# A hybrid decoder layer on Trainium2: modulation chunks computed inside the projections, and another order of the prompt attention inside the sample attention

## The chip, the cores and the metric

The kernel runs on one core of a Trainium2 chip. The metric is the device time of one execution in microseconds (us). Its engines are TensorE (PE, with its weight loads as PEld), VectorE (DVE), ScalarE (ACT), GpSimd (POOL) and SyncE (SP), which here only issues transfers. Sixteen DMA engines move the data.

## What is computed

One layer for a prompt of 512 tokens and, beside it, for 8 sequences of 8 sample tokens with 2048 cached positions each. The width is 1024.

```python
mod = (jax.nn.silu(c) @ w_ada + b_ada).reshape(B, 6, 1, D_MODEL)
shift1, scale1, gate1, shift2, scale2, gate2 = [mod[:, i] for i in range(6)]
h = x * (1 + scale1) + shift1
proj = h @ w_in                      # 1024 x 3072: qa, ka, va, qb, kb, vb
qa, ka, qb, kb = rope(...)           # 64 columns per head
oa, win_state = attend_a(qa, ka, va)
ob = rms_norm(attend_b(qb, kb, vb, lam), subln_g) * (1.0 - lam_init)
mixed = concat(oa, ob) @ w_o
x = layer_norm(ALPHA * x + gate1 * mixed)
h = x * (1 + scale2) + shift2
x = layer_norm(ALPHA * x + gate2 * conv_ffn(h))
```

`attend_a` has 8 heads of 64; each query sees keys at three patterns of window and dilation, (128, 1), (512, 4) and (2048, 16), and the three results are mixed by their softmax sums. `attend_b` has 4 heads with two query and key maps of 64 and a value of 128: softmax(q1 k1) v minus lambda times softmax(q2 k2) v. The sample tokens read window caches (A) and a paged cache through a page table (B). The window caches, shifted by 8 rows, are outputs too: 16 copies from memory to memory (keys and values of 8 sequences), 4 MB each.

## The kernel before

All engines are programmed by hand, each with its own list of instructions, in order; they wait for one another by semaphores. `x_sb`, `ht`, `ring` and `room` are large regions of on-chip memory, each divided anew stage by stage; `wide` is the matmul output memory, `bk(i)` one of its eight banks of 512 columns.

**Weights** are cut into 37 chunks of 2 MB (128 partitions x 8 x 512), listed in `CHUNKS` (L42), and go through slots of `ring` by `SLOT_OF` (L44). SyncE loads them with `load_chunk` (L460, the transfer at L482), which waits until the slot's last chunk is used. A chunk of `w_ada` gives 512 of the 6144 modulation columns, for 9 rows of c. TensorE multiplies it in `ada_rows` (L1516; eight matmuls of 512 columns, L1524), VectorE copies the product (L1026), TensorE sums and transposes it in `ada_sum` (L1528; four matmuls of 9 columns, L1536), VectorE adds the bias (L1031).

**Stage 1, projections.** After modulation chunks 0 to 3 (shift and scale of the first half) come 30 units (s, t): six chunks s of `w_in` by five token tiles t (4 of the prompt, 1 of the sample). TensorE does a unit in `product` (L1573 to L1577), in three parts because numbers are split into a high part and a rest; VectorE and GpSimd split the weights (L1065 to L1080 and L701), VectorE rotates queries and keys (rope, L1122), GpSimd adds (L715). TensorE transposes queries and keys (L1626); ScalarE copies the queries into `qtp` (L834), where each head has its own 128 rows of which 64 are zero (GpSimd writes the zeros at the start, L673), and the values into `vp` (L827). SyncE walks the units too: it stores the new keys and values (L536, L540, L551, L554), and after the last tile of a chunk loads the next `w_in` chunk and, for the first three, copies a window pair (`move_window`, L515 to L517); one more pair is copied ahead of the units. When the units are done it loads modulation chunks 4 to 11 through three ring slots.

**Stage 2, prompt attention of head group A.** A unit is a head and a block of 128 queries: 32 units for A, in a pipeline of four steps: scores (TensorE, L1636), mask and minimum (VectorE, L1164), exponential (ScalarE, L844), transposes (TensorE, L1643), copy (VectorE, L1172), weighing with the values (TensorE, L1649), scaling (VectorE, L1183). In steps with s % 4 == 3 stands an `ada_rows`, in those behind them the `ada_sum`:

```python
if s % 4 == 0 and s >= 4:
    ada_sum(4 + s // 4 - 1)
...
if s < NU and s % 4 == 3:
    ada_rows(4 + s // 4)
```

In the last four steps VectorE begins to turn (transpose in blocks of 32, `turn_keys`, L1148) the key groups of the first window.

**Stage 3, sample attention.** 16 windows w: for each of 8 sequences first cache A (3 groups), then cache B (4 groups). SyncE and GpSimd's queue bring key groups into 3 buffers (`kraw`, L589, L592, L596) and value groups into 4 (`vg`, L445, L453). The 8 new rows of keys and values of a window lie in `kn` and `vn`, two buffers each, loaded by `load_new` (L422 to L426): for windows 0 and 1 by ScalarE when the prompt attention is over, later by SyncE. VectorE turns them in `turn_new` (L1230). TensorE scores each group (`score_group`, L1700), VectorE takes minima, ScalarE exponentials, and `weigh_group` (L1732) sums. Between them lie the 32 prompt units of head group B, two for each window, in three parts on each engine: `scores_b`, `turn_b`, `weigh_b` (TensorE, L1674 to L1687), `mask_b`, `out_b` (VectorE, L1203 to L1224), `probs_b`, `copy_b` (ScalarE, L853 to L869). Their order is written out in the loop over the windows: scores of unit 2w at the start, transposes of 2w and scores of 2w + 1 after value group 2, weighing of 2w and transposes of 2w + 1 at the end, weighing of 2w + 1 at the start of the next.

**After it**: the norm of B's rows, the output projection, both layer norms, and the ConvFFN, with the remaining window copies.

## Time and profile before

| | us |
|---|---|
| median of 3 runs | 1243.8 (1243.23 to 1244.69) |
| the profiled execution | 1241.13 |
| its span, first to last instruction | 1239.0 |
| TensorE busy | 1055.3 (85%) |
| VectorE busy | 838.9 (68%) |
| GpSimd busy | 358.1 (29%) |
| ScalarE busy | 269.6 (22%) |
| moved by DMA | 276.5 MB, mean 223 GB/s |

The profile is that of one execution. Its busy shares are averages over the span; the page's slices and the windows of the trace give them by stretch, with the granted TensorE clock (1.00 is 2.4 GHz, 0.50 is 1.2 GHz). The stages lie at 0 to 51.8 (start and first modulation), 51.8 to 237.1 (projections), 237.1 to 310.4 (prompt attention of group A), 310.4 to 649.6 (sample attention) and from there to 1239.0.

### The profile page before, as it was taken

How to read it: one execution, taken by the hardware profiler on the slowest of the kernel's cores; microseconds unless marked ns; L12 is line 12 of the kernel's file. 1: busy time of each engine (PE TensorE's matmuls, PEld its weight loads, DVE VectorE, ACT ScalarE, POOL GpSimd, SP SyncE). 2: the span in 40 equal slices, each digit the busy share in tenths (PEclk: the TensorE clock that was granted, in tenths of full speed). 3: DMA queues.
4: the chain of work that ended last, by engine and by line, in shares of the span. 5: the costliest groups of instructions: out<-in, count | busy, mean ns of one | idle time of the engine just before them, and what ended most of it. 6: DMA issues, size and time to landing. Idle time of an engine off the chain costs nothing.

```text
span 1239.0 us, 24009 instructions
## 1 busy us (share of the span) xinstructions
PE 1055.3 (85%) x9389; PEld 851.3 (69%) x9389; DVE 838.9 (68%) x1521; ACT 269.6 (22%) x588; POOL 358.1 (29%) x378
## 2 busy tenths in 40 slices
PE   4599999999577777766785996999999999999994
PEld 2377777666455545554564875999999999777772
DVE  1657457267766757685749477477676676998958
ACT  0310010232223223232333103322332232100002
POOL 2433243100000000000007005366565565434323
PEclk9799999999788679799876996999999999999997
DMA  8958894686999999999990206366567731412202
GB/s 301 403 185 303 309 370 145 215 302 225 318 325 339 313 346 302 343 331 350 301 334 17 64 26 221 121 252 238 204 221 285 269 107 69 148 56 97 73 22 77
DMA packets 112549, 276.54 MB, mean 223 GB/s; under 512 B 9608, under 2 KB 33174, under 8 KB 108837
## 3 DMA queue, kind: packets, MB, share of 16 engines
q1 hardware_dynamic: 99125, 250.82, 59.8%
q10 hardware_dynamic: 13312, 24.19, 5.5%
q8 instruction: 75, 1.23, 0.4%
q14 instruction: 37, 0.30, 0.1%
HBM read 264.60 MB, written 76.69 MB: 275 GB/s over the span
## 4 chain that ended last, share of the span: by engine, by line
PE 61%; DVE 21%; DMA 9%; issue 4%; SPq 3%; POOL 2%; ACT 1%; ACTq 0%; DVEq 0%; POOLq 0%; PEldq 0%
PE wide L1575 16%; PE wide L1577 15%; PE wide L1576 15%; DMA ring<-in_cache_k 5%; DVE ring L1148 5%; PE wide L1649 3%; PE wide L1638 2%; DMA ring<-in_w_ada 2%; PE wide L1700 2%; DVE ring_r L1080 2%; PE wide L1732 1%; PE wide L1524 1%; DMA ring<-in_w_down 1%; PE wide L1754 1%; PE wide L1643 1%
## 5 line engine op out<-in xcount | busy, mean ns | idle before, releaser
L744 POOL TENSOR_TENSOR ring_r<-ring,ring_r 128x1024 fp32r<-128x1024 f32 x70 | 185.2, 2654 | 271.1 <-DVE ring_r L1040 204.2
L1575 PE MATMUL wide<-x_sb_r,ring_r 128*128 128x288 f32 x704 | 211.4, 300 | 8.2 <-DVE ht_r L1062 5.1
L1576 PE MATMUL wide<-ht_r,ring_r 128*128 128x288 f32 x704 | 209.3, 297 | 0.0
L1577 PE MATMUL wide<-x_sb_r,ring_r 128*128 128x288 f32 x704 | 208.7, 296 | 0.0
L1577 PE MATMUL wide<-ring_r,ht_r 128*128 128x512 f32 (+1 forms) x400 | 158.9, 397 | 0.0
L1148 DVE STREAM_TRANSPOSE ring<-ring 128x512 f32<-128x512 f32 x208 | 129.2, 674 | 30.4 <-DMA ring<-in_cache_k 30.4
L1575 PEld LDWEIGHTS wide<-x_sb_r,ring_r 128*128 128x128 f32 x704 | 133.4, 189 | 11.7 <-issue 11.2
L1577 PEld LDWEIGHTS wide<-x_sb_r,ring_r 128*128 128x128 f32 x704 | 134.2, 191 | 0.0
L1576 PEld LDWEIGHTS wide<-ht_r,ring_r 128*128 128x128 f32 x704 | 133.7, 190 | 0.0
L1700 PE MATMUL wide<-ring,x_sb 128*32 128x128 f32 (+1 forms) x1792 | 70.2, 309 | 50.5 <-DVE ring L1148 50.4
L1575 PE MATMUL wide<-ring_r,x_sb_r 128*128 128x512 f32 (+1 forms) x240 | 97.7, 407 | 12.1 <-DVE ht_r L1062 10.1
L1700 PEld LDWEIGHTS wide<-ring,x_sb 128*32 128x32 f32 x1792 | 52.9, 127 | 69.7 <-DVE ring L1148 61.6
L726 POOL COPY x_sb<-ring 32x128 f32<-32x128 f32 x64 | 18.4, 287 | 269.0 <-PE wide L1700 266.8
L1576 PE MATMUL wide<-ring_r,x_sb_r 128*128 128x512 f32 (+1 forms) x240 | 94.9, 395 | 0.0
L1575 PE MATMUL wide<-ring_r,ht_r 128*128 128x512 f32 (+1 forms) x220 | 88.1, 400 | 4.4 <-DVE ht_r L1400 2.5
L1577 PEld LDWEIGHTS wide<-ring_r,ht_r 128*128 128x128 f32 (+1 forms) x400 | 72.4, 181 | 21.5
L1576 PE MATMUL wide<-ring_r,ht_r 128*128 128x512 f32 (+1 forms) x220 | 86.6, 394 | 0.0
L1414 DVE SCALAR_TENSOR_TENSOR room<-room,vec_t 128x512 f32<-128x512 f32 x44 | 56.9, 1294 | 40.4 <-ACT room L957 40.2
L949 ACT ACTIVATE room<-wide,vec_t 128x576 f32<-128x576 f32 x44 | 32.8, 744 | 205.9 <-PE wide L1577 201.2
L1416 DVE SCALAR_TENSOR_TENSOR room<-room,vec_t 128x512 f32<-128x512 f32 x44 | 71.5, 1625 | 1.6
L1040 DVE CAST ring_r<-ring 128x1024 fp32r<-128x1024 f32 x62 | 41.9, 687 | 35.9 <-DMA ring<-in_w_up 29.4
L1649 PE MATMUL wide<-room 128*128 128x128 f32 x320 | 57.2, 315 | 9.6 <-ACT room L869 8.4
(225 smaller groups left out, 1889.0 us busy)
## 6 DMA issues: line engine op xcount, KB each, us to landing
ring<-in_cache_k SPq DMA_DIRECT2D x128, 256.0 KB
out_wks<-in_cache_win_k SPq DMA_DIRECT2D x8, 4080.0 KB, 19.0
out_wvs<-in_cache_win_v SPq DMA_DIRECT2D x8, 4080.0 KB, 24.8
ring<-in_w_ada SPq DMA_DIRECT2D x12, 2048.0 KB, 10.2
ring<-in_w_up SPq DMA_DIRECT2D x22, 1024.0 KB, 7.3
ring<-in_cache_win_k SPq DMA_DIRECT2D x16, 1024.0 KB
ring<-in_w_in SPq DMA_DIRECT2D x6, 2048.0 KB, 18.5
room<-in_cache_v ACTq DMA_DIRECT2D x32, 256.0 KB
```

The lines of the kernel that those rows point to most:

```text
L744: nc.gpsimd.tensor_tensor(rest, w, high.bitcast(F32), ALU.subtract).then_inc(wl_rest, 1)
L949: nc.scalar.activation(u_b[:, k % 2, 2:2 + NT].rearrange("p (h t) -> p h t", h=2), pair, ACT.Identity, bias=vec_t[:, 0, 48 + f:49 + f]).th ...
L1040: nc.vector.tensor_copy(pair_of(n, slice(k, k + 2))[0], slot(SLOT_OF[n])[:, k:k + 2, :]).then_inc(wl_high, 1)
L1080: nc.vector.tensor_tensor(rest, w, high.bitcast(F32), ALU.subtract).then_inc(win_dve, 1)
L1148: last = nc.vector.transpose(ktg[:, G % NK, :, 32 * t:32 * t + 32], kraw[G % NK][:, t, :].rearrange("p (g d) -> p g d", d=32))
L1414: then(nc.vector.scalar_tensor_tensor(out=c_p, in0=u_b[:, k % 2, 1:1 + SEQ], scalar=tap(1), in1=c_p, op0=ALU.mult, op1=ALU.add))
L1416: nc.vector.scalar_tensor_tensor(out=c_p, in0=u_b[:, k % 2, 0:SEQ], scalar=tap(0), in1=c_p, op0=ALU.mult, op1=ALU.add)
L1575: nc.tensor.matmul(out, left[0], right[0], start=first, stop=False)
L1576: nc.tensor.matmul(out, left[0], right[1], start=False, stop=False)
L1577: return nc.tensor.matmul(out, left[1], right[0], start=False, stop=last)
L1649: last = nc.tensor.matmul(bank[:, 0:P], pt_b[:, u % 2, P * kb:P * kb + P], vp[:, kb, m, P * (n // 2):P * (n // 2) + P], start=(kb == 0), s ...
L1700: last = nc.tensor.matmul(bank[32 * nn:32 * nn + 32, at:at + nk], qbd[:, w % 2, g].rearrange("p i q -> p (i q)"), keys[:, g, 0:nk], start= ...
```

## The change

- The eight late modulation chunks leave the weights ring and the prompt attention. They go one after the other through a buffer of their own, `late`, in `room`, and their products stand ahead of units 3, 6, 10, 13, 16, 20, 23 and 26 of the projections (`LATE_UNIT`), each sum one unit later. SyncE asks for a chunk with `load_late` once the product before has been made, after the stores of the unit at which that product stands.
- The 8 window copies of the projections are spread singly over the units (`COPY_UNIT`).
- The queries lie in `qt` with two heads' 64 rows one above the other; scores are made with 64 rows. The 8192-column memset goes, ScalarE copies a tile's queries with one instruction. The space gives `late` its place, and value buffers 2 and 3 of the sample attention lie there afterwards.
- `kn`, `vn` and `ktn` have one buffer each. The first window's new rows are loaded by ScalarE ahead of its first exponential, those of later windows by SyncE, keys and values by separate steps.
- As before 32 prompt units (group A) precede the sample attention and 32 (group B) lie in it, but there each of the 34 `prompt_step(y)` does the weighing of y - 2, the transposes of y - 1 and the scores of y, at the start of a window and after its value group 1. ScalarE's and VectorE's parts move accordingly.

```diff
-CHUNKS = [("ada", i) for i in range(4)] + [("in", i) for i in range(6)] + [("ada", i) for i in range(4, 12)] \
+CHUNKS = [("ada", i) for i in range(4)] + [("in", i) for i in range(6)] \
     + [("o", i) for i in range(2)] + [("up", i) for i in range(11)] + [("down", i) for i in range(6)]
-SLOT_OF = [0, 1, 2, 3] + [0, 1] * 3 + [0, 1, 2, 0, 1, 2, 0, 1] + [i % 2 for i in range(19)]
+SLOT_OF = [0, 1, 2, 3] + [0, 1] * 3 + [i % 2 for i in range(19)]
...
+LATE_UNIT = {4: 3, 5: 6, 6: 10, 7: 13, 8: 16, 9: 20, 10: 23, 11: 26}
+COPY_UNIT = {1: (0, "k"), 4: (0, "v"), 8: (1, "k"), 11: (1, "v"), 14: (2, "k"), 18: (2, "v"), 21: (3, "k"), 24: (3, "v")}
...
-        qtp = part(room, 0, 8192).rearrange("p (n t) -> p n t", n=16)
-        kt = part(room, 8192, 4096).rearrange("p (f t) -> p f t", f=8)
...
+        late = part(room, 12288, KT_D * CH).rearrange("p (k n) -> p k n", k=KT_D)
+        qt = part(room, 0, 4096).rearrange("p (f t) -> p f t", f=8)
+        kt = part(room, 4096, 4096).rearrange("p (f t) -> p f t", f=8)
+        vp = part(room, 8192, 4096).rearrange("p (m t d) -> p t m d", t=TP, m=2)
...
-              for t, at in ((x_flat, 0), (x_flat, 2048), (room, 0), (room, 2048))]
+              for t, at in ((x_flat, 0), (x_flat, 2048), (room, 12288), (room, 14336))]
...
-            eng.dma_start(kn[0:DS, w % 2, :], k_s[DS * b:DS * b + DS, m, :]).then_inc(new_in[w % 2], 16)
-            eng.dma_start(vn[0:DS, w % 2, :], v_s[DS * b:DS * b + DS, m, :]).then_inc(new_in[w % 2], 16)
+            eng.dma_start(kn[0:DS, :], k_s[DS * b:DS * b + DS, m, :]).then_inc(kn_in, 16)
...
+            eng.dma_start(vn[0:DS, :], v_s[DS * b:DS * b + DS, m, :]).then_inc(vn_in, 16)
...
+            def load_late(ch):
...
+                if ch > 4:
+                    sp.wait_ge(ada_mm, ch)
+                src = a["w_ada"][0].rearrange("(k p) n -> p k n", p=P)
+                sp.dma_start(late, src[:, :, CH * ch:CH * ch + CH]).then_inc(late_in, 16)
...
-            sp.wait_ge(ada_ok, 4)
-            move_window(0)
+            load_late(4)
...
                 if t == TP:
-                    load_chunk(6 + s)
-                    if s < 3:
-                        move_window(s + 1)
-            for n in range(12, 18):
-                load_chunk(n)
+                    if s < 4:
+                        load_chunk(6 + s)
+                for ch, at in LATE_UNIT.items():
+                    if at == n and ch < 11:
+                        load_late(ch + 1)
+                if n in COPY_UNIT:
+                    i, which = COPY_UNIT[n]
+                    move_window(i, (("cache_win_k", "wks") if which == "k" else ("cache_win_v", "wvs"),))
...
-            load_values(sp, 0, 0)
-            load_values(sp, 0, 1)
-            sp.wait_ge(w_used, CHUNK_AT[("ada", 9)] + 1)
+            sp.wait_ge(w_used, CHUNK_AT[("in", 4)] + 1)
...
                     if G == 2:
-                        sp.wait_ge(pa_min, NU)
+                        sp.wait_ge(ada_mm, 12)
...
                     if G == 2:
-                        sp.wait_ge(w_used, CHUNK_AT[("ada", 11)] + 1)
+                        sp.wait_ge(w_used, CHUNK_AT[("in", 5)] + 1)
+                        load_values(sp, 0, 0)
+                        load_values(sp, 0, 1)
...
+                if w >= 1:
+                    sp.wait_ge(kn_t, w)
+                    load_new_keys(sp, w)
                 if w >= 2:
-                    sp.wait_ge(kn_t, w - 1)
                     sp.wait_ge(sa_pv, w - 1)
-                    load_new(sp, w)
+                    load_new_values(sp, w - 1)
...
-            nc.gpsimd.memset(qtp, 0.0).then_inc(qzero, 1)
...
+            for i, place in enumerate((kn, ktn)):
+                nc.gpsimd.memset(place, 0.0).then_inc(new_zero, 1)
+                pool.wait_ge(new_zero, i + 2)
...
-                if w == 1:
-                    pool.wait_ge(q_bd, 2)
-                    pool.wait_ge(pa_min, NU)
-                    for i, place in enumerate((kn, ktn, small)):
-                        nc.gpsimd.memset(place, 0.0).then_inc(new_zero, 1)
-                        pool.wait_ge(new_zero, i + 1)
...
-                    m0 = 8 * (s // 3)
-                    for h in range(2):
-                        last = nc.scalar.activation(qtp[64 * h:64 * h + 64, m0 + h:m0 + 8:2, P * t:P * t + P],
-                                                    src[64 * h:64 * h + 64], ACT.Copy)
-                    last.then_inc(qk_a, 1)
+                    m0 = 4 * (s // 3)
+                    nc.scalar.activation(qt[:, m0:m0 + 4, P * t:P * t + P], src, ACT.Copy).then_inc(qk_a, 1)
...
+            act.wait_ge(new_zero, 3)
+            act.wait_ge(rope_ok, len(rope_units))
+            act.wait_ge(pj_a, len(v_units))
+            load_new_keys(act, 0)
+            load_new_values(act, 0)
             for u, (m, n, qb) in enumerate(pa[:NU]):
...
-            act.wait_ge(pa_o, NU)
-            act.wait_ge(out_sem, 16 * (TP * 2 + 2 * DB + 2))
-            act.wait_ge(new_zero, 3)
-            load_new(act, 0)
-            load_new(act, 1)
...
-                probs_b(2 * w)
+                probs_b(PER * w)
+                if w:
+                    copy_b(PER * w - 1)
...
                     load_values(act, w + 1, 1)
+                probs_b(PER * w + 1)
+                copy_b(PER * w)
                 if values_by_act(w + 1, 2):
                     load_values(act, w + 1, 2)
-                copy_b(2 * w)
-                probs_b(2 * w + 1)
                 act.wait_ge(sa_pv, w + 1)
                 nc.scalar.activation(o_s[:, w, :], bk(4)[:, 0:P], ACT.Copy).then_inc(sa_o, 1)
-                copy_b(2 * w + 1)
+            copy_b(len(pb) - 1)
...
+            jobs += [(n - 0.5, "late_rows", ch) for ch, n in LATE_UNIT.items()]
+            jobs += [(n + 0.55, "late_sum", ch) for ch, n in LATE_UNIT.items()]
             dve.wait_ge(rope_in, 16)
             for _, what, n in sorted(jobs):
+                if what == "late_rows":
+                    ada_rows(n)
+                    continue
+                if what == "late_sum":
+                    ada_sum(n)
+                    continue
...
-                if s % 4 == 0 and s >= 4:
-                    ada_sum(4 + s // 4 - 1)
...
-                if s < NU and s % 4 == 3:
-                    ada_rows(4 + s // 4)
...
-            dve.wait_ge(w_used, CHUNK_AT[("ada", 11)] + 1)
...
             def turn_new(w):
-                dve.wait_ge(new_in[w % 2], 32 * (w // 2 + 1))
-                if w >= 2:
-                    dve.wait_ge(sa_s, w - 1)
...
+                dve.wait_ge(kn_in, 16 * (w + 1))
+                if w >= 1:
+                    dve.wait_ge(sa_s, w)
...
+                mask_b(PER * w)
+                if w:
+                    out_b(PER * w - 2)
...
                     turn_keys(w + 1, 1)
-                if w:
-                    out_b(2 * w - 1)
-                mask_b(2 * w)
                 if last_g:
                     turn_keys(w + 1, 2)
+                mask_b(PER * w + 1)
+                if w:
+                    out_b(PER * w - 1)
                 if last_g == 4:
                     turn_keys(w + 1, 3)
-                mask_b(2 * w + 1)
                 if last_g:
                     turn_new(w + 1)
...
-                landed(n)
+                if ch < 4:
+                    landed(CHUNK_AT[("ada", ch)])
+                else:
+                    pe.wait_ge(late_in, 16 * (ch - 3))
+                w = slot(SLOT_OF[CHUNK_AT[("ada", ch)]]) if ch < 4 else late
...
+                for c, at in LATE_UNIT.items():
+                    if at == n - 1:
+                        ada_sum(c)
+                    if at == n:
+                        ada_rows(c)
...
-                return nc.tensor.matmul(bank[:, 0:P * (qb + 1)], qtp[:, 8 * m + n, P * qb:P * qb + P],
-                                        kt[:, 4 * m + n // 2, 0:P * (qb + 1)], start=True, stop=True)
+                at = slice(64 * (n % 2), 64 * (n % 2) + 64)
+                return nc.tensor.matmul(bank[:, 0:P * (qb + 1)], qt[at, 4 * m + n // 2, P * qb:P * qb + P],
+                                        kt[at, 4 * m + n // 2, 0:P * (qb + 1)], start=True, stop=True)
...
-                if s % 4 == 0 and s >= 4:
-                    ada_sum(4 + s // 4 - 1)
...
-                if s < NU and s % 4 == 3:
-                    ada_rows(4 + s // 4)
...
+            def prompt_step(y):
+                if y >= 2:
+                    weigh_b(y - 2)
+                if 1 <= y <= len(pb):
+                    turn_b(y - 1)
+                if y < len(pb):
+                    scores_b(y)
...
-                if w:
-                    weigh_b(2 * w - 1)
-                scores_b(2 * w)
+                prompt_step(PER * w)
...
-                    if g == 2:
-                        turn_b(2 * w)
-                        scores_b(2 * w + 1)
-                pe.wait_ge(new_in[w % 2], 32 * (w // 2 + 1))
+                    if g == 1:
+                        prompt_step(PER * w + 1)
+                pe.wait_ge(vn_in, 16 * (w + 1))
...
                 last.then_inc(sa_pv, 1)
-                weigh_b(2 * w)
                 if nxt:
                     score_new(w + 1)
-                turn_b(2 * w + 1)
-            weigh_b(2 * len(sa) - 1)
+            prompt_step(len(pb))
+            prompt_step(len(pb) + 1)
```

**TensorE, a round of the prompt attention, before.** From the scores of one four-block unit over the product of the next modulation chunk (`wide<-ring,c_t`) and its sum (`wide<-sum,ht`) to the next round's second scores.

```order
L1638 MATMUL wide<-room 128x512
L1643 MATMUL wide<-ident,room 128x128 x2
L1649 MATMUL wide<-room 128x128
L1524 MATMUL wide<-ring,c_t 9x512 x8
L1638 MATMUL wide<-room 128x128
L1643 MATMUL wide<-ident,room 128x128 x3
L1536 MATMUL wide<-sum,ht 128x9 x4
L1649 MATMUL wide<-room 128x128 x2
L1638 MATMUL wide<-room 128x256
```

After, the same stretch:

```order
L1675 MATMUL wide<-room 128x512
L1680 MATMUL wide<-ident,room 128x128 x2
L1686 MATMUL wide<-room 128x128
L1675 MATMUL wide<-room 128x128
L1680 MATMUL wide<-ident,room 128x128 x3
L1686 MATMUL wide<-room 128x128 x2
L1675 MATMUL wide<-room 128x256
```

The product and the sum are gone; the scores, transposes and weighings keep their order.

**SyncE's queue around the fourth projection chunk, before**: the window copies (`out_wks<-in_cache_win_k` and `out_wvs<-in_cache_win_v`), the stores of new keys and values, and the weights.

```order
L517 DMA out_wks<-in_cache_win_k 64x16320
L517 DMA out_wvs<-in_cache_win_v 64x16320
L536 DMA out_wkp<-mix 128x512 x4
L540 DMA out_wks<-ring 8x512 x8
L482 DMA ring<-in_w_in 128x8x512
L517 DMA out_wks<-in_cache_win_k 64x16320
L517 DMA out_wvs<-in_cache_win_v 64x16320
L551 DMA out_wvp<-room 128x512 x4
L554 DMA out_wvs<-ring 8x512 x8
```

After:

```order
L556 DMA out_wkp<-mix 128x512 x2
L534 DMA room<-in_w_ada 128x8x512
L556 DMA out_wkp<-mix 128x512 x2
L538 DMA out_wks<-in_cache_win_k 64x16320
L560 DMA out_wks<-ring 8x512 x8
L496 DMA ring<-in_w_in 128x8x512
L571 DMA out_wvp<-room 128x512
L534 DMA room<-in_w_ada 128x8x512
L571 DMA out_wvp<-room 128x512
L538 DMA out_wvs<-in_cache_win_v 64x16320
L571 DMA out_wvp<-room 128x512 x2
L534 DMA room<-in_w_ada 128x8x512
```

Each 4 MB window copy stands alone between stores; in this stretch three late modulation chunks (`room<-in_w_ada`) are asked for, the middle one a store behind the weights of `w_in`.

**ScalarE, from the last projections to the prompt attention, before.** The value copies, then the exponentials; the loads of the new rows stood behind the last of 32 exponentials.

```order
L827 ACTIVATE room<-wide 128x512 x4
L827 ACTIVATE ring<-wide 64x512
L844 ACTIVATE room,rs<-room,mn 128x128
L844 ACTIVATE room,rs<-room,mn 128x256
L844 ACTIVATE room,rs<-room,mn 128x384
```

After:

```order
L849 ACTIVATE room<-wide 128x512 x4
L849 ACTIVATE ring<-wide 64x512
L437 DMA ht<-ring 8x512
L442 DMA ht<-ring 8x512
L868 ACTIVATE room,rs<-room,mn 128x128
L868 ACTIVATE room,rs<-room,mn 128x256
L868 ACTIVATE room,rs<-room,mn 128x384
```

The two loads (`ht<-ring`) of the first window's new rows now stand ahead of the first exponential.

## Rows read from the trace of the kernel before

**Rows 1.** The chain of waits, the whole span, by engine.
```profile
PE 61%; DVE 21%; DMA 9%; issue 4%; SPq 3%; POOL 2%; ACT 1%; ACTq 0%; DVEq 0%; POOLq 0%; PEldq 0%
```

**Rows 2.** Windows: stretch, length, PE, PEld, DVE, ACT, POOL, PEclk, DMA share, GB/s.
```profile
51.80:237.10 185.30, 178.78 (x792) 135.36 (x792) 103.33 (x168) 16.21 (x28) 60.29 (x45) 0.98 0.74 258
237.10:310.40 73.30, 69.92 (x496) 47.12 (x496) 51.84 (x185) 20.86 (x64) 4.95 (x12) 1.00 0.76 272
310.40:649.60 339.20, 245.80 (x4693) 178.60 (x4694) 225.75 (x596) 92.57 (x299) 16.08 (x56) 0.81 1.01 327
```

**Rows 3.** Timeline, TensorE, one prompt attention round: start, duration, instruction.
```profile
266.65 1.90 PE L1524 MATMUL wide<-ring,c_t 128*9 128x512 f32 x16
268.49 0.49 PE L1638 MATMUL wide<-room 128*128 128x128 f32 x2
...
269.42 1.03 PE L1536 MATMUL wide<-sum,ht 128*128 128x9 f32 x8
270.30 0.69 PE L1649 MATMUL wide<-room 128*128 128x128 f32 x4
...
275.42 1.91 PE L1524 MATMUL wide<-ring,c_t 128*9 128x512 f32 x16
```

**Rows 4.** Groups of instructions, 237.1 to 310.4: busy us, mean ns, idle before.
```profile
L1643 PE MATMUL wide<-ident,room 128*128 128x128 f32 x80 | 14.0, 273 | 0.0
...
L1026 DVE COPY ht<-wide 128x512 f32<-128x512 f32 x8 | 5.5, 691 | 6.5 <-PE wide L1524 6.5
```

**Rows 5.** Timeline, VectorE, end of the prompt attention.
```profile
300.79 1.29 DVE L1148 STREAM_TRANSPOSE ring<-ring 128x512 f32<-128x512 f32 x2
...
310.18 1.30 DVE L1148 STREAM_TRANSPOSE ring<-ring 128x512 f32<-128x512 f32 x2
```

**Rows 6.** Timeline, TensorE at unit 10, ScalarE's copies of units 10 to 12.
```profile
117.59 0.47 PE L1575 MATMUL wide<-ring_r,x_sb_r 128*128 128x512 f32 x1
...
124.14 0.60 ACT L827 ACTIVATE room<-wide 128x512 f32<-128x512 f32 x1 [29.59 <-PE wide L1577]
130.07 0.60 ACT L827 ACTIVATE room<-wide 128x512 f32<-128x512 f32 x1 [5.33 <-PE wide L1577]
135.51 0.60 ACT L827 ACTIVATE room<-wide 128x512 f32<-128x512 f32 x1 [4.84 <-PE wide L1577]
```

**Rows 7.** Timeline, SyncE, row stores of unit 9.
```profile
125.60 2.68 SPq L540 DMA_DIRECT2D out_wks<-ring  x8
```

**Rows 8.** DMA issues, 80 to 95: KB each, us from issue to landing.
```profile
out_wks<-in_cache_win_k SPq DMA_DIRECT2D x1, 4080.0 KB, 20.0
...
ring<-in_w_in SPq DMA_DIRECT2D x1, 2048.0 KB, 8.1
```

**Rows 9.** Timeline, GpSimd and ScalarE around the prompt attention's start and end.
```profile
236.59 0.95 POOL L719 MEMSET x_sb<- 128x1024 f32 x1 [21.18 <-PEq L1611]
...
238.15 0.40 ACT L844 ACTIVATE room<-room,mn 128x128 f32<-128x128 f32 x1 [1.24 <-DVE mn L1164]
...
310.33 1.30 ACTq L425 DMA_DIRECT2D room<-ring  x1
...
311.66 0.68 ACTq L426 DMA_DIRECT2D ht<-ring  x1
```

**Rows 10.** Timeline, VectorE, first new rows of the sample attention.
```profile
314.57 0.70 DVE L1234 STREAM_TRANSPOSE room<-room 32x512 f32<-32x512 f32 x1 [3.10 <-DMA ht<-ring]
```

**Rows 11.** Windows, three stretches of the sample attention, columns as in rows 2.
```profile
375.00:385.00 10.00, 9.42 (x93) 6.31 (x94) 6.36 (x18) 3.69 (x9) 1.15 (x4) 0.50 1.06 320
433.00:443.00 10.00, 7.06 (x152) 4.63 (x140) 5.82 (x20) 3.58 (x14) 1.15 (x4) 1.00 1.05 387
322.00:324.00 2.00, 2.00 (x44) 1.63 (x45) 1.62 (x4) 0.54 (x2) 0.00 (x0) 0.61 0.60 122
```

**Rows 12.** Timeline, TensorE, first scores after a wait.
```profile
374.90 1.51 PE L1700 MATMUL wide<-ring,x_sb 128*32 128x128 f32 x24 [4.48 <-DVE ring L1148]
```

**Rows 13.** Waits of VectorE, 326 to 643: us in all, times, longest.
```profile
DVE room L1215 <- PE wide L1649: 27.0, 15, 3.1
```

80 lines of the change are left out of this document (44 added, 36 removed).

## Prediction

> **What bounds the kernel now.** I read the page's chain of waits first, then the time by stage, then each stage's own view. The chain is 61% TensorE and only 9% DMA [rows 1], but that is an average over stages with different limits. By stage [rows 2]: in the six projections TensorE is busy 178.8 of 185.3 us and the DMA engines 0.74 of the time; in the first prompt attention (32 units) TensorE is busy 69.9 of 73.3 us; in the sample attention it is busy 246 of 339 us, while the DMA share is 1.01 at 327 GB/s. So TensorE bounds the first two, the transfers of keys and values the third. The change does not touch what comes after 649.6 us.
>
> Two consequences. TensorE work moved from the prompt attention into the projections moves between two stages with the same bound, so it pays only where it now causes waits. And what the change does to the order inside the sample attention pays only where the DMA engines stand idle.
>
> **Late modulation leaves the prompt attention.** One round of four units lasts 8.77 us, from one product of modulation rows to the next (266.65 to 275.42) [rows 3]. In it the product takes 1.84 us (266.65 to 268.49) and its transposed sums 0.88 (269.42 to 270.30), on the path, since TensorE is in order and full. Between 268.49 and 269.42 TensorE has one 128-column score and three transposes, and the sums wait for VectorE's copy of the product (0.69 us each, [rows 4]); I count 0.3 us of waiting there. A round without it: 8.77 − 1.84 − 0.88 − 0.3 = 5.75 us. VectorE has some 5.2 us of work in a round, so it doesn't take over. Seven rounds give 7 × 3.02 = 21.1 us. In the last one VectorE also turns the first key groups between 300.79 and 310.18 [rows 5] and is itself full, so only its copy and its small addition go there: 0.9. Gain **22.0 us**; the ends are 17 (VectorE sets a round of 6.4) and 24.
>
> **It enters the projections.** A projection unit takes 5.44 us (130.07 to 135.51) [rows 6]. Eight products and sums cost 8 × (1.84 + 0.88) = **21.8 us**, all of it on the path, as TensorE is busy 96% here. Two of them fall on holes: unit 10 takes 6.55 us up to its copy where a clean one takes some 5.65 [rows 6], since it waits for the splitting of its weights by VectorE and GpSimd. The products stand directly ahead of units 10 and 20, each the first of a chunk, so that much is hidden twice: **−1.7 us**. VectorE's share, 8 × (0.69 + 0.20) = 7 us, costs nothing: it is busy 103 of 185 us; if the splits came late by it, TensorE would wait about 1 us per chunk.
>
> **The single buffer of the late weights.** Each chunk of 2 MB is asked for when the product before it is done, and on SyncE behind the stores of the unit it stands at. The tight place is chunk 7. SyncE reaches it after the eight row stores of unit 9, which start at 125.60 and take 2.68 us [rows 7], and behind projection chunk 3: 128.3 in the old time. A lone chunk lands 8.1 us after its issue [rows 8]; a second right behind it at 387 GB/s [rows 11] 5.4 us later, with a store between, 142.5. TensorE wants it ahead of unit 13: unit 10 began at 117.59 [rows 6], plus 1.84 for product 6, three units of 5.44, one sum of 0.88 and the transposes of 0.4: 137.0. So it waits **5.0 us** (I take off 0.5 for a chunk that lands sooner; ends 0 and 8). A pause like this has a second price: after 4.48 us without work at 370.4 [rows 12] the granted clock of the next ten microseconds is 0.50 [rows 11], the 1.2 GHz level. Four to five microseconds of units at half clock cost **2 us** (0 to 4.5). The other late chunks I reckon from the same rows, with a 4 MB window copy at 20.0 − 8.1 = 12 us [rows 8] ahead of them: chunks 8, 10 and 11 land 0 to 2 us before they are wanted, the rest 8 or more. The projections' DMA share of 0.74 has room for the 15 MB (seven of the eight chunks; the first was already loaded here): they are 38 us of transfer in 185 × 0.26 = 48 idle ones plus the 25 us by which the stage grows.
>
> **The start of the prompt attention.** ScalarE now issues the first new rows' two loads ahead of its first exponential, which began at 238.15 [rows 9]. It waits for GpSimd's two memsets of 512 columns, half of the 0.95 us that 1024 take, begun at 236.59, then needs 0.65 to 1.30 us per issue [rows 9]. The first exponential moves to about 239.5, and the second transpose step with it: **+1.3 us**. Queries without zero halves: the 64-row score streams the same columns, so nothing on TensorE; ScalarE's copies halve and the 8192-column memset goes, both off the path: zero (between −1 and +1 for 32 scores).
>
> **The sample attention.** Its first new keys are there already. Before, VectorE waited 3.10 us for them (314.57) [rows 10] and everything behind moved with it, down to the next key loads, in front of which the DMA engines ran at 122 GB/s and share 0.60 (322 to 324) [rows 11]: **−2.5 us**. The rest of the stage is bound by transfers: 13.6 MB for each pair of windows at 387 GB/s where the traffic is dense, slower for the loads that fill 32 partitions. Stretches like that at 322 are short and few after it, some 5 us in all by a walk through the windows; I give the new order of the prompt units, which takes VectorE's waits for weighing (27.0 us in 15 times, [rows 13]) largely away, **−2 us** of that (ends +8 and −13: a new-row load of values that is asked for one window later than before could hold TensorE, or the transfers could follow the engines). The tail keeps its length: the last three prompt steps already ran one behind the other there.
>
> Sum: 21.8 − 1.7 + 5.0 + 2 − 22.0 + 1.3 − 2.5 − 2 = +1.9 us. The profiled execution took 1241.13 us (span 1239.0), 2.7 below the median of 1243.8; against it this is 1243.0, against the median **1245.7 us**: no difference that a measurement can tell, which I put at 0.2% or 2.5 us.
>
> **A rule against the change.** In the prompt attention transposes are 14.0 us of TensorE's time [rows 4] and the clock is 1.00 [rows 2]; the products of modulation, 8 × 1.84 = 14.7 us, are what leaves, and the scores that stay use half the rows. The Trainium skill (TensorE: Matmul & The Clock Gate, Part 4: PE-mode transpose) says that transposes do not count as busy for the clock gate. By that rule the stage loses part of what keeps its clock up; the trace neither agrees nor disagrees, because it never shows the stage without the products. If the clock fell, a round of 5.7 us of TensorE work would take 11.4.
>
> **Rivals.**
> - *The late loads are in time* (0.22): SyncE gets to chunk 7 sooner or the two chunks share the engines well. Without the 5.0 and the 2: 1238.7 us. For it: the stage's transfers are not dense at 120 to 130 in the old time; against it: the order in which SyncE meets its waits.
> - *The transfers of the sample attention follow the engines* (0.13): the load of a key group is asked for when VectorE has turned an older one, so that shorter waits bring transfers forward. Half of the 27.0 us of [rows 13] gone: 1245.7 − 13.5 + 2 = 1234. Against it: share 1.01.
> - *Window copies in front of the late chunks make TensorE wait three or four times more* (0.18), slower than before: it decides if a chunk lands over 2 us later than reckoned, as the 4 MB copies are put into the queue just ahead of chunks 8, 10 and 11. Three waits of 3 us, each with 1 us of low clock: +12, 1258 us.
> - *The prompt attention falls to the low clock* (0.05): half of the eight rounds at 11.4 instead of 5.8 us is +22: 1268 us. Against it: what stays is mostly scores and weighings, without gaps between them.
>
> **How the numbers follow.** Forecast 0.42, own range 1241 to 1250. Faster by over 0.2%: 0.03 of it, 0.17 of the first rival, all 0.13 of the second: 0.33. Within 0.2%: 0.24 and 0.05: 0.29. Slower: 0.15, 0.18 and 0.05: 0.38. The range 1232 to 1258 leaves out the last rival and the outer parts of the second and third.
>
> **What would show it.** A prompt round of 5.8 us; the projections longer by 20 us plus waits, TensorE idle for a late chunk once, ahead of unit 13, some 5 us, with clock 0.5 behind it; the first exponential 1 to 1.5 us late; no wait for new keys at the first window; the sample attention within 5 us of its length at DMA share 1.0. I am wrong if the sample attention changes by over 8 us, if a prompt round stays above 6.5, or if no TensorE wait names the late chunk.

## The result, and the profile after

The changed kernel takes **1283.99 us** (median of 4 executions, 1260.27 to 1301.73), the kernel before 1243.51 (1241.46 to 1244.69); the ratio is 1.0187 with a 95% interval of 1.0098 to 1.0275, so the change is slower; whether by more than 2% is left open. It is outside the forecast's range of 1232 to 1258. Its executions lie 41 us apart where those of before lie 3 apart. This ratio and those below take only the executions within 1.5% of their kernel's fastest, here the two shorter ones, so they understate a kernel that scatters; the scatter is part of what has to be explained. The profiled execution took 1272.71 us (span 1270.6).

The page's chain of waits by engine, of the changed kernel (before: [rows 1]):

```profile
PE 63%; DVE 17%; DMA 8%; issue 5%; SPq 3%; ACT 1%; POOL 1%; ACTq 1%; DVEq 0%; PEldq 0%; POOLq 0%
```

TensorE has gained two points of the chain and VectorE lost four, though the stage with most of VectorE's waits is as long as it was. The windows of the changed kernel, with the columns of [rows 2]: projections, prompt attention, sample attention, the rest.

```profile
51.80:266.42 214.62, 203.16 (x985) 146.23 (x985) 109.93 (x186) 11.38 (x20) 59.29 (x45) 0.96 0.82 294
266.42:342.54 76.12, 70.94 (x305) 46.83 (x305) 45.59 (x169) 20.83 (x64) 3.77 (x10) 0.78 0.21 72
342.54:679.49 336.95, 252.47 (x4684) 184.59 (x4685) 225.56 (x593) 87.94 (x297) 16.07 (x56) 0.78 1.01 327
679.49:1270.60 591.11, 537.63 (x3272) 478.00 (x3271) 440.31 (x541) 130.16 (x181) 262.99 (x257) 0.95 0.39 136
```

| stage (boundaries by the same instructions) | before | after | forecast | measured |
|---|---|---|---|---|
| projections | 185.4 | 214.6 | +27.1 | +29.2 |
| prompt attention | 73.3 | 76.1 | -20.7 | +2.8 |
| sample attention | 338.1 | 336.9 | -4.5 | -1.2 |
| rest | 590.4 | 591.1 | 0 | +0.7 |
| span | 1239.0 | 1270.6 | +1.9 | +31.6 |

The projections came out nearly as reckoned. The loss is in the prompt attention: TensorE has the granted clock 0.78 there instead of 1.00, and its 71 us of busy time are no less than the 70 of before, although eight products and sums have left. Two windows of that stage show how it goes:

```profile
270.10:304.20 34.10, 34.10 (x104) 22.34 (x104) 14.68 (x57) 7.89 (x25) 0.48 (x2) 0.50 0.35 122
304.25:340.00 35.75, 33.44 (x186) 22.40 (x186) 27.39 (x101) 12.00 (x36) 0.00 (x0) 1.00 0.00 1
```

From 270.1 to 304.2 the clock is 0.50 (1.2 GHz), with TensorE busy all of that time, then 1.00 to the end of the stage with the same kinds of instructions. A round of four units takes 12.6 us at the low clock (282.51 to 295.13) and 6.86 at the high one (312.97 to 319.83). At the stage's start, first TensorE, then ScalarE (timelines of the changed kernel; TensorE's L1675 is a score, L1680 a transpose; ScalarE's L437 and L442 are the loads of the first new rows):

```profile
266.42 1.85 PE L1675 MATMUL wide<-room 64*128 64x128 f32 x6 [0.88 <-ACT ring L849]
269.70 0.33 PE L1680 MATMUL wide<-ident,room 128*128 128x128 f32 x1 [1.44 <-ACT room L868]
269.96 2.00 PE L1675 MATMUL wide<-room 64*128 64x512 f32 x2
```
```profile
267.02 1.38 ACTq L437 DMA_DIRECT2D ht<-ring  x1
268.43 0.68 ACTq L442 DMA_DIRECT2D ht<-ring  x1
269.16 0.40 ACT L868 ACTIVATE room<-room,mn 128x128 f32<-128x128 f32 x1 [3.00 <-issue]
```

The first exponential begins at 269.16, 2.7 us behind the first score (1.0 before: 237.16 and 238.15), and TensorE stands still 1.44 us for it. Then the score at 269.96 already runs slowly. And in the projections, SyncE's queue and TensorE around the forecast's "tight place":

```profile
134.74 0.41 SPq L496 DMA_DIRECT2D ring<-in_w_in  x1
...
135.81 0.43 SPq L534 DMA_DIRECT2D room<-in_w_ada  x1
```
```profile
148.93 3.60 PE L1554 MATMUL wide<-room,c_t 128*9 128x512 f32 x16 [4.95 <-DMA room<-in_w_ada]
```
```profile
150.00:155.00 5.00, 5.00 (x20) 2.23 (x13) 0.69 (x1) 0.00 (x0) 0.00 (x0) 0.60 1.14 408
```

TensorE waits 4.95 us for late chunk 7, as forecast (5.0), and the clock behind it is low (0.60 in 150 to 155; the product itself takes 3.60 us instead of 1.90).

### The profile page after: what moved, and what is told of

The parts are those of the page before. It is cut to its first block, busy times and chain, and to the rows that moved or that the text cites. A ratio compares the mean times of both kernels' runs of the same rounds, so it can differ in the third digit from the quotient of the medians.

```text
span 1270.6 us, 23984 instructions
## 1 busy us (share of the span) xinstructions
PE 1091.0 (86%) x9389; PEld 870.0 (68%) x9389; DVE 837.9 (66%) x1521; ACT 261.0 (21%) x580; POOL 349.4 (27%) x377
## 4 chain that ended last, share of the span: by engine, by line
PE 63%; DVE 17%; DMA 8%; issue 5%; SPq 3%; ACT 1%; POOL 1%; ACTq 1%; DVEq 0%; PEldq 0%; POOLq 0%
PE wide L1606 16%; PE wide L1607 15%; PE wide L1608 15%; DMA ring<-in_cache_k 4%; DVE ring L1177 3%; PE wide L1742 3%; PE wide L1675 3%; PE wide L1686 2%; PE wide L1774 2%; DMA ring<-in_w_ada 2%; PE wide L1680 1%; PE wide L1554 1%; PE wide L1793 1%; DMA ring<-in_w_down 1%; SPq L619 1%
## 5 line engine op out<-in xcount | busy, mean ns | idle before, releaser
L1606 PE MATMUL wide<-x_sb_r,ring_r 128*128 128x288 f32 x704 | 211.3, 300 | 10.6 <-DVE ht_r L1083 7.5
L1177 DVE STREAM_TRANSPOSE ring<-ring 128x512 f32<-128x512 f32 x208 | 128.5, 672 | 26.2 <-DMA ring<-in_cache_k 11.3
L1742 PE MATMUL wide<-ring,x_sb 128*32 128x128 f32 (+1 forms) x1792 | 74.7, 322 | 34.1 <-DVE ring L1177 31.4
L1742 PEld LDWEIGHTS wide<-ring,x_sb 128*32 128x32 f32 x1792 | 56.1, 132 | 53.9 <-DVE ring L1177 36.7
L1686 PE MATMUL wide<-room 128*128 128x128 f32 x320 | 60.1, 327 | 8.1 <-ACT room L888 4.0
```

Of the source, the lines that this page charges most:

```text
L1177: last = nc.vector.transpose(ktg[:, G % NK, :, 32 * t:32 * t + 32], kraw[G % NK][:, t, :].rearrange("p (g d) -> p g d", d=32))
L1606: nc.tensor.matmul(out, left[0], right[0], start=first, stop=False)
L1686: last = nc.tensor.matmul(bank[:, 0:P], pt_b[:, u % 2, P * kb:P * kb + P], vp[:, kb, m, P * (n // 2):P * (n // 2) + P], start=(kb == 0), s ...
L1742: last = nc.tensor.matmul(bank[32 * nn:32 * nn + 32, at:at + nk], qbd[:, w % 2, g].rearrange("p i q -> p (i q)"), keys[:, g, 0:nk], start= ...
```

## The experiments

Four questions: does the pause at the start bring the clock down; do the 64-row scores; what do they cost by themselves; and why is the late chunk late. Theory 1 stands for the pause, theory 2 for what is left in the stage (64-row scores, no products). Each kernel ran beside the kernel before on the same chip, but not all groups of experiments on one chip: a1, d1, b1 and c1 belong together, then f1, f4 and f2, then k0, k1, h1 and h2, then i1 and i2.

### The loads put behind the exponentials

ScalarE's three waits for them move along.

```diff
-            load_new_keys(act, 0)
-            load_new_values(act, 0)
             for u, (m, n, qb) in enumerate(pa[:NU]):
...
             act.wait_ge(pa_pv, NU)
+            load_new_keys(act, 0)
+            load_new_values(act, 0)
```

> The changed kernel, with ScalarE's two loads of the first new rows put back behind its 32 exponentials. Theory 1 (the pause): TensorE stood still for 0.88 and 1.44 us at 265.3 to 269.7 because the first exponential waited for these loads, and the granted clock was 0.50 from 270 to 302; without the second pause the clock stays at 1.00, the rounds of four units take 5.8 to 6.5 us instead of 12.6, and the time falls by 15 to 20 us against the changed kernel's profiled 1272.7, to about 1253 to 1258. Theory 2 (what is left in the stage): scores of 64 rows and no products do not hold the clock; the stage still has 0.50 for 20 to 30 us and the time stays at 1268 to 1275.

Measured: 1255.07 us (1254.09, 1254.70, 1255.43, 1271.34), ratio 1.0153 (1.0074 to 1.0233). Window and timeline of this kernel, the prompt attention and one round of four units:

```profile
266.75:325.80 59.05, 55.31 (x305) 36.99 (x306) 45.02 (x169) 20.85 (x64) 3.79 (x10) 1.00 0.27 92
```
```profile
291.01 0.49 PE L1675 MATMUL wide<-room 64*128 64x128 f32 x2
...
297.87 0.49 PE L1675 MATMUL wide<-room 64*128 64x128 f32 x2
```

In the profiled execution the clock holds at 1.00 and the stage takes 59.05 us, 17 less. That looked like theory 1. But the round is 6.86 us (291.01 to 297.87), not 5.75, and one execution of four took 16 us more.

### The same pause in the kernel before

```diff
+            act.wait_ge(q_bd, 2)
             for u, (m, n, qb) in enumerate(pa[:NU]):
```

> The kernel before, whose first exponential also waits until GpSimd has laid out the queries of the first two windows, which makes TensorE's second pause 1.7 us longer, as in the changed kernel. Theory 1 (the pause): the granted clock falls to 0.50 in the prompt attention here too, products or not; the stage grows by 20 us or more, to some 1265. Theory 2: the clock stays at 1.00, and the time grows by the 1.7 us alone, to 1245.

Measured: 1243.16 us (10 executions, 1240.40 to 1246.78) beside 1241.89, ratio 1.0015 (0.9991 to 1.0038). The stage:

```profile
239.67:314.99 75.32, 70.14 (x496) 47.06 (x497) 51.94 (x185) 20.84 (x64) 4.86 (x12) 1.00 0.74 265
```

75.3 us instead of 73.3, clock 1.00. TensorE's second pause is 1.78 us long, and it costs about its own length and no clock. Theory 1 in its plain form has fallen.

### 64-row scores in the kernel before

```diff
-                return nc.tensor.matmul(bank[:, 0:P * (qb + 1)], qtp[:, 8 * m + n, P * qb:P * qb + P],
+                at = slice(64 * (n % 2), 64 * (n % 2) + 64)
+                return nc.tensor.matmul(bank[:, 0:P * (qb + 1)], qtp[at, 8 * m + n, P * qb:P * qb + P],
```

> The kernel before, whose prompt scores use only the 64 rows that are not zero, all else as it was. If 64-row scores (part of theory 2) cost the clock, the granted clock falls below 1.00 in the prompt attention and the time grows by 5 us or more. Theory 1 and the prediction's zero for this part: the same clock, the same 8.77 us per round, 1243.8 within 2.5 us.

Measured: 1252.28 us (6 executions, 1244.50 to 1256.72) beside 1241.89, ratio 1.0072 (1.0034 to 1.0110): **+10 us for this part alone**, which the forecast had at zero. The clock is 1.00 in the profiled execution, so both theories miss what it costs. TensorE's timeline with 64 rows, from the four-block score of one round to the product of the next, then the same in the kernel before:

```profile
260.74 1.90 PE L1524 MATMUL wide<-ring,c_t 128*9 128x512 f32 x16
...
267.90 1.06 PE L1650 MATMUL wide<-room 128*128 128x128 f32 x8
268.89 1.12 PE L1639 MATMUL wide<-room 64*128 64x512 f32 x2
269.94 0.44 PE L1644 MATMUL wide<-ident,room 128*128 128x128 f32 x2
270.22 0.39 PE L1650 MATMUL wide<-room 128*128 128x128 f32 x2
270.53 1.90 PE L1524 MATMUL wide<-ring,c_t 128*9 128x512 f32 x16
```
```profile
264.36 1.06 PE L1649 MATMUL wide<-room 128*128 128x128 f32 x8
265.26 1.02 PE L1638 MATMUL wide<-room 128*128 128x512 f32 x2
266.12 0.38 PE L1643 MATMUL wide<-ident,room 128*128 128x128 f32 x2
266.33 0.39 PE L1649 MATMUL wide<-room 128*128 128x128 f32 x2
```

With 128 rows the score begins 0.90 us behind the weighing, the transposes 0.86 behind the score, the next weighing 0.21 behind them. With 64 rows the three steps take 0.99, 1.05 and 0.28: 0.35 us more around this score, and less around the shorter ones. A round takes 9.79 us (260.74 to 270.53) instead of 8.77 [rows 3]: four scores, 1.02 us, about **0.25 us for each 64-row score between 128-row matmuls**. Eight rounds are 8.2 us; in the profiled execution the stage went from 73.3 to 81.0. The sample attention with its 32 prompt scores went from 338.1 to 344.4, but that is not shown to be the scores': its length differs from 336 to 346 us over the profiles here, 345.5 among them with 128 rows (i1).

TensorE's weight loads (PEld) around the same score say where the time goes, first with 64 rows, then with 128:

```profile
268.89 0.29 PEld L1639 LDWEIGHTS wide<-room 64*128 64x128 f32 x2
269.94 0.20 PEld L1644 LDWEIGHTS wide<-ident,room 128*128 128x128 f32 x2 [0.76 <-ACT room L844]
```
```profile
265.15 0.30 PEld L1638 LDWEIGHTS wide<-room 128*128 128x128 f32 x2
265.69 0.14 PEld L1643 LDWEIGHTS wide<-ident,room 128*128 128x128 f32 x1 [0.24 <-issue]
```

With 128 rows the score's weights are loaded from 265.15, ahead of the score (265.26) and beside the weighing, and those of the first transpose from 265.69, in the middle of the score. With 64 rows both loads begin only with their own matmul (268.89 and 269.94); the exponentials that the last one could have waited for had ended by 269.15. So in these rows a load is hidden behind the matmul ahead of it only where both have 128 rows.

### The products put back as matmuls nobody uses

```diff
+                if s < NU and s % 4 == 3:
+                    for k in range(KT_D):
+                        j = k % 4
+                        nc.tensor.matmul(bk(6)[32 * j:32 * j + C, :], c_t[:, k, :], kt[:, k, :],
+                                         start=(k < 4), stop=(k >= 4))
```

> The changed kernel plus eight matmuls of 9 x 512 columns in each of the eight rounds of the prompt attention, with nobody using what they give (the work of the products that left, without their loads and sums). Theory 1 (the pause): the clock falls after the same pause, and the stage is longer by the products at half clock, some 8 x 1.84 = 15 us or up to 25: about 1288 to 1297. Theory 2 (what is left does not hold the clock): the products hold it, at 1.00, as before; the rounds take 5.8 + 1.84 = 7.6 us instead of 12.6 and the time falls to 1260 or below.

Measured: 1273.50 us (1269.11 to 1275.18), ratio 1.0251 (1.0208 to 1.0295). Windows: two at the start, and the stage.

```profile
270.06:275.06 5.00, 5.00 (x21) 1.26 (x20) 1.40 (x5) 0.81 (x2) 0.00 (x0) 0.51 1.01 391
275.06:280.06 5.00, 5.00 (x34) 3.66 (x31) 3.41 (x14) 1.22 (x5) 0.00 (x0) 1.00 1.05 318
265.06:341.53 76.47, 72.79 (x432) 40.38 (x433) 46.30 (x169) 20.84 (x64) 3.77 (x10) 0.96 0.22 72
```

The clock falls behind the same pause, and it falls at 268.1, before the first of the added products:

```profile
271.80 3.43 PE L1708 MATMUL wide<-room,c_t 128*9 128x512 f32 x16
```

At 274.9, while that product ends, the clock is back at 1.00, 6.8 us after the fall; the four executions lie within 6 us of each other, so none can have stayed low for long. The time is more than theory 2 gave (I had left the 64-row cost out: rounds of 8.69 us, not 7.6), and less than theory 1's. With the products the clock came back soon; the fall they could not have prevented, since they stand behind it.

### All 128 rows in the changed kernel, without and with the pause

```diff
-                at = slice(64 * (n % 2), 64 * (n % 2) + 64)
+                at = slice(0, P)
```

> The changed kernel with the two loads behind the exponentials and with scores made from all 128 rows of the query store, so that each of the 64 prompt units gets the scores of two heads added up (this part of the result is another one; the instructions and their columns are those of scores with zero halves). Theory 3 (64-row scores cost about 0.13 us at each change between 64 and 128 rows): the round of the prompt attention falls from 6.86 to 5.83 us, the stage by 8 us, and the time from 1255 to about 1245. Rival: the extra 1.0 us of a round in the kernel before with 64 rows came from the layout of its store; then 1255 stays.

> The changed kernel with all 128 rows in its prompt scores (the scores of two heads added up, another result) and the loads left ahead of the first exponential, so with the pause. Theory 1 (the pause alone): the clock falls to 0.50 as in the changed kernel, a stage of about 68 us, 1262 or more. Theory 2b (64-row scores do not hold the clock, 128-row scores do): the clock stays at 1.00 or comes back within 10 us; 1247 to 1252.

Measured: 1249.92 us (1246.04 to 1254.11), ratio 1.0074 (1.0011 to 1.0137), with the loads behind; 1254.09 (1250.32 to 1256.04), ratio 1.0103 (1.0042 to 1.0164), with the pause. The stage in each:

```profile
264.52:317.21 52.69, 48.69 (x304) 38.14 (x305) 43.77 (x169) 20.88 (x64) 3.77 (x10) 0.95 0.32 107
```
```profile
266.26:320.62 54.36, 48.23 (x305) 37.51 (x305) 43.78 (x169) 20.84 (x64) 3.77 (x10) 0.97 0.31 103
```

52.7 and 54.4 us: the forecast's 52.6, and the clock is 1.00 without products, pause or not, up to the last 5 us of the stage, where VectorE sets the pace. A round takes 5.89 us (284.00 to 289.89 in f1) instead of 6.86, near the 5.83 expected, and the rival about the store's layout is out; the stage is 6.4 us shorter than a1's, not 8, and the time 1249.92, not 1245. So neither the pause nor the missing products is enough; every fall at this stage's start was seen with 64-row scores.

### The change and the moved loads once more, side by side

> The changed kernel once more, unaltered, beside the next one on the same chip: how long the granted clock stays at 0.50 in the prompt attention. Theory 2b (prompt attention with 64-row scores and without products stands at the edge, and falls or not from one execution to the next; with the pause nearly always): the stage is 60 to 120 us long from one execution to another, the times scatter over 20 us or more, above 1260. Theory 1 (the pause decides): all executions close together near 1272.

> The changed kernel with the loads behind the exponentials, once more, on the same chip as the changed kernel itself. Theory 1 (the pause decides): 1255 again in all executions. Theory 2b: at least one execution above 1265, with a low clock in the prompt attention although TensorE never stands still there.

Measured: the change 1261.45, 1292.13, 1293.03, 1295.97 us; the loads behind 1250.05, 1259.01, 1271.06, 1297.80. Windows of the profiled execution of each (1295.97 and 1271.06):

```profile
270.00:275.00 5.00, 5.00 (x16) 3.04 (x15) 2.40 (x10) 1.59 (x6) 0.00 (x0) 0.50 1.01 392
345.00:350.00 5.00, 5.00 (x15) 3.05 (x15) 2.30 (x9) 1.07 (x3) 0.00 (x0) 0.50 0.00 0
```
```profile
270.00:275.00 5.00, 5.00 (x19) 3.90 (x20) 2.43 (x9) 1.33 (x6) 0.00 (x0) 0.50 1.01 406
305.00:310.00 5.00, 5.00 (x32) 3.65 (x32) 4.24 (x19) 2.00 (x7) 0.00 (x0) 1.00 0.00 0
```

In the first the clock is 0.50 from 268.7 to 354.0, most of a stage of 99.3 us, with TensorE busy all the time; in the second from 268.0 to 302.1, in a stage of 74.6. In the second TensorE had no pause of 1.44 us. The scatter is theory 2b's: the change gets a stage of 76.1 or 99.3 us, the same kernel with the loads behind one of 59.1 (a1) or 74.6 (k1).

### The late chunk: product moved, copies moved, asked for sooner

Product 7 ahead of unit 14 and product 8 ahead of 17 (`LATE_UNIT = {..., 7: 14, 8: 17, ...}`):

> The changed kernel with the loads behind the exponentials, and the products of late chunks 7 and 8 ahead of units 14 and 17 instead of 13 and 16. Theory 4 (the prediction's: the wait of 4.95 us ahead of unit 13 for chunk 7, with clock 0.79 to 0.87 behind it, is a matter of the place): no wait for a late chunk, the projections 6 to 7 us shorter than 215.0, the time 1248 to 1250 against 1255. Rival: the transfers are the limit there and the wait moves to chunk 8 or to the next weights; 1253 to 1256.

Measured: 1294.77 us (1277.45 to 1303.22), ratio 1.0388 (1.0292 to 1.0484). TensorE at late chunk 8, and the clock in the prompt attention:

```profile
174.59 1.90 PE L1554 MATMUL wide<-room,c_t 128*9 128x512 f32 x8 [5.34 <-DMA room<-in_w_ada]
```
```profile
270.00:280.00 10.00, 10.00 (x33) 6.90 (x33) 4.92 (x19) 2.02 (x7) 0.86 (x3) 0.50 1.03 397
340.00:350.00 10.00, 10.00 (x30) 6.29 (x30) 3.99 (x18) 2.02 (x6) 0.00 (x0) 0.50 0.00 0
```

The wait is now 5.34 us for the next chunk, and the projections take 215.0 us as before; the rival was right. The 40 us on top are again the clock, 0.50 from 269.2 to 361.4. Of 64-row kernels without products this was the slowest; whether its other spacing has a part in that, or chance, its four executions cannot say.

Three window copies moved from the projections to behind the third key group:

> The changed kernel with the loads behind the exponentials and three of the eight window copies (those of units 11 to 21) moved out of the projections to behind the third key group, into the prompt attention, where the DMA engines moved next to nothing for 35 us. Theory 4 (late chunk 7 is late because SyncE's list puts it behind stores and its transfer beside window copies and projection weights): the wait ahead of unit 13 shrinks from 4.95 to 1 to 3 us, and the projections by 3 to 5 us from 215.0; with the clock at 1.00 the time is 1250 to 1252. Rival: the chunk is late because it is asked for late; the wait stays near 5 us, the time 1255.

> As the last kernel, with all 128 rows in the prompt scores too (scores of two heads added up, another result). If the three causes (64-row scores 8 us and the fragile clock, the pause, the wait for a late chunk) are what separates the change from the forecast, nothing but the forecast's own sum is left: prompt attention 52 to 53 us, projections 208 to 212, 1241 to 1246 beside a kernel before of 1238 to 1243.

Measured: 1257.72 us (1252.78 to 1264.61), ratio 1.0142 (1.0086 to 1.0198), with 64 rows; 1252.10 (7 executions, 1246.76 to 1257.88), ratio 1.0102 (1.0072 to 1.0132), with 128. The second was expected at 1241 to 1246, so of what separates the change from the forecast something is still missing: its projections took 213.4 us (208 to 212 expected), its prompt attention 52.6 as expected, and its profiled execution (1246.76) is its shortest, so the rest is open. SyncE's queue and TensorE in the first:

```profile
135.90 0.41 SPq L496 DMA_DIRECT2D ring<-in_w_in  x1
...
136.97 0.43 SPq L534 DMA_DIRECT2D room<-in_w_ada  x1
```
```profile
149.96 2.75 PE L1557 MATMUL wide<-room,c_t 128*9 128x512 f32 x12 [4.81 <-DMA room<-in_w_ada]
```

The DMA share of the projections fell from 0.82 to 0.66, and the wait stayed at 4.81 us. Chunk 7 is asked for 1.1 us behind the fourth projection chunk; they landed 12.9 and 8.0 us after their requests, in the changed kernel 13.1 and 8.2. So the window copies moved away here are not the reason, and what is left is when the chunk is asked for. In the last pair SyncE asks one unit sooner, ahead of that unit's stores:

```diff
             for n, (s, t) in enumerate(units):
+                for ch, at in LATE_UNIT.items():
+                    if at == n + 1 and ch < 11:
+                        load_late(ch + 1)
...
-                    if at == n and ch < 11:
```

> The changed kernel with the loads behind the exponentials and all 128 rows in the prompt scores (the scores of two heads added up, another result), in which SyncE asks for each late chunk one unit sooner, ahead of that unit's stores. Chunk 7 is then asked for when product 6 is done, at about 128 instead of 136, and ahead of the fourth projection weights. If it is late because it is asked for behind the stores: no wait ahead of unit 13, projections 206 to 208 instead of 212.7 to 213.4, and 6 us less than the 1250 to 1252 of the two like kernels. Rival: the projection weights become late instead, or the transfer itself takes 13 us wherever it starts; the projections stay at 213.

> As the last one with the true 64-row scores, so the whole computation: the best form of the change as it stands. Projections 206 to 208; prompt attention 59 where the clock holds and 75 to 100 where it falls, so executions between 1244 and 1290, the median above the kernel before in any case.

Measured: with 128 rows **1245.78 us** (10 executions, 1241.75 to 1252.42) beside 1241.33, ratio 1.0029 (0.9995 to 1.0063); with the true 64 rows 1268.30 (6 executions, 1251.30 to 1291.77), ratio 1.0209 (1.0138 to 1.0281). SyncE's request, TensorE's remaining wait, and the first two stages of the former:

```profile
125.94 0.40 SPq L534 DMA_DIRECT2D room<-in_w_ada  x1
```
```profile
166.65 2.17 PE L1554 MATMUL wide<-room,c_t 128*9 128x512 f32 x12 [2.61 <-DMA room<-in_w_ada]
```
```profile
51.80:263.07 211.27, 202.25 (x985) 145.92 (x985) 109.76 (x185) 11.43 (x20) 59.80 (x45) 0.97 0.83 298
263.07:315.19 52.12, 47.09 (x304) 36.76 (x305) 43.77 (x169) 20.87 (x64) 3.78 (x10) 1.00 0.31 105
```

Asked for at 125.94, chunk 7 lands 15.1 us later, at 141.0, and TensorE does not wait for it; its transfer took no less time, it only began sooner. 2.61 us of waiting are left, ahead of unit 16 for chunk 8, which is asked for at 145.68, 6 us behind a window copy, and takes 20.9 us. The projections fell to 211.3, from 212.7 (f1) and 213.4 (h2) in the two like kernels: less than I expected (206 to 208). The ratio fell from 1.0074 and 1.0102 to 1.0029, by more than these 1.4 to 2.1 us; the interval overlaps f1's, the chips differ, and the profiled execution (1252.42) is the slowest of the ten, with a sample attention of 345.5 us, so that part is not explained. With the true 64 rows the profile (1260.51) has a prompt attention of 60.5 us, with the clock low for 3.4 us at its start only.

## Why the prediction was wrong, point by point

**What bounds the kernel** held: projections bound by TensorE, the sample attention by transfers at a share of 1.01 before and after.

**The projections** (+27.1 forecast, +29.2 measured) held: TensorE is busy 24.4 us longer (21.8 for products and sums, 2 for the low clock forecast), its waits for GpSimd's splits, 1.6 us before, are gone (1.7 forecast), and the late chunk's wait is 4.95 for 5.0, at the unit named, clock 0.60 behind it. Not reckoned: the first unit starts at 54.36 instead of 51.78, of which 1.5 us are left at its next wait (58.06 against 56.56). The forecast put the tightness on when SyncE gets to the request, and i1 bears that out for chunk 7.

**"Queries without zero halves ... nothing on TensorE"** is the first step that failed. It rested on the streamed columns being the same, and they are; but each 64-row score among 128-row matmuls takes 0.25 us more, and b1's trace has the weight loads around it no longer hidden: 7.7 us in the prompt attention of the kernel before (81.0 in b1 against 73.3), 6.4 in that of the changed one (59.05 in a1 against 52.69 in f1), outside the ends of -1 and +1 that I gave. No row of before showed a matmul with other than 128 rows next to one with 128 in this stage, so a range of a few tenths for each of 32 scores would have been due.

**"The prompt attention falls to the low clock" (0.05)** is the second, and the larger. The rival was named and its price (+22) right in size: the clock was low for 34 us in the profiled execution, which with the pause is 76.1 - 59.05 = 17 us, and up to 40 in others. I gave it 0.05 because "what stays is mostly scores and weighings, without gaps between them". Once it was up the clock did hold (through the 59 us of a1, and the last 38 of the changed kernel's stage), but the absence of gaps did not bring it back: TensorE was busy without one through 34 us at 0.50. And the stage does have gaps, at its start: some 0.9 us ahead of the first score in every kernel, and with the pause 1.44 more. Every profiled fall lies within 2.4 to 3.7 us of that first score. The executions by what the prompt attention has in it:

| prompt scores | products | pause | executions, us | profiled: clock low from the stage's start |
|---|---|---|---|---|
| 128 rows | yes | no (before) | 49: 1232 to 1252 | no |
| 128 rows | yes | yes (d1) | 10: 1240 to 1247 | no |
| 64 rows | yes | no (b1) | 6: 1244 to 1257 | no |
| 64 rows | yes | yes (c1) | 4: 1269 to 1275 | 6.8 us |
| 128 rows | no | no (f1, h2, i1) | 21: 1242 to 1258 | no, in all three |
| 128 rows | no | yes (f4) | 4: 1250 to 1256 | no |
| 64 rows | no | no (a1, h1, i2, k1, f2) | 22: 1250 to 1303 | no, no, 3.4, 34, 92 us |
| 64 rows | no | yes (change, k0) | 8: 1260 to 1302 | 34, 85 us |

With 128 rows no profile shows such a fall and no execution is above 1258 us; with 64 rows it falls in six of nine profiles, and with the products it was back after 6.8 us where without them it took 3 to 92. So the falls went with the 64-row scores, and the products' part that shows is the return; the change takes both away at once. Whether the products also make the fall rarer, b1's six executions cannot say: a fall as short as c1's would not stand out in them. Nor is it shown that the pause makes it likelier: above 1265 us are 6 of 8 executions with it and 11 of 22 without.

The prediction weighed the Trainium skill (TensorE: Matmul & The Clock Gate, Part 4: PE-mode transpose), by which transposes don't count as busy for the gate. The kernels with 128 rows have the same transposes and no products either and are at 1.00 until the last 5 us of the stage at least: what tips it here is the height of the scores, of which that section says nothing. Whether the height acts through how busy the array is, or through the weight loads that no longer hide, no run tells apart.

**The first exponential** was forecast 1 to 1.5 us late and was 1.7 late.

**A prompt round** (5.75 forecast) takes 5.89 us where the rows are full and the clock is up: the waiting around the sums, put at 0.3, was 0.16, 1 us over seven rounds. With 64 rows it is 6.86, and 12.6 at the low clock; that a prompt round "stays above 6.5" was one of the prediction's own signs of being wrong.

**The sample attention** (-4.5, measured -1.2): the wait for the first new rows went, as forecast. VectorE's waits for weighing [rows 13] went too, and its waits for cache keys fell from 30.4 us to 11.3; in their place it waits longer for prompt scores (35.1 us, 22.5 before) and for sample scores (33.9, 2.5 before). Two of these rows of the changed kernel's sample attention:

```profile
DVE room L1227 <- PE wide L1675: 35.1, 15, 5.4
...
DVE ring L1177 <- DMA ring<-in_cache_k: 11.3, 7, 3.2
```

Before, the stage took 338.1 us. With the new order and 128 rows it takes 338.6 (f1), 340.1 (f4), 336.7 (h2) and 345.5 (i1), with 64 rows 336.4 (a1) to 345.2 (f2), one profiled execution each. So the new order is worth nothing that shows; the -2 us forecast for it and the -2.5 us for the first wait are smaller than this scatter.

The sum of 29.7 us missed in the profiled execution: projections 2.1, prompt attention 23.5 (6.4 of 64-row scores, a1 against the forecast's 52.6, and 17.1 of clock with its pause, the change against a1), sample attention 3.3, rest 0.7. With the 64 rows, the pause and the wait for chunk 7 taken away (i1, whose prompt scores are those of two heads added up) the ratio is 1.0029, where the forecast was +1.9 us or 1.0015. No version found here beats the kernel before: TensorE's work was moved from one TensorE-bound stage to another, and the 54 us in which the DMA engines then stood idle (share 0.21 in the prompt attention) brought nothing in. That the key and value buffers were full then is my reading of the kernel, not measured.

## What to carry to other kernels

Moving work between two stages with the same bound buys nothing, and it can uncover what the work had been doing for the stage that it left: here, bringing the clock back soon after a fall. Where a change removes dense matmuls and makes the rest shorter in rows at once, undo each by itself before judging either, and look at the scatter of the executions: a clock that falls in some and not in others shows there first. When a chunk is late by some microseconds, look first at what its request stands behind in the issuing engine's list, and only then at its traffic.
